# Modulation products on four column tiles of TensorE, six blocks summed in one PSUM bank, and the result turned by a product with a constant

## The reference

```python
for i in range(DEPTH):                      # second block, DEPTH = 2
    mod_l = (silu(c) @ w_mod[i] + b_mod[i]).reshape(b, 9, 1, 1024)
    mod_c = (silu(c_ctx) @ w_mod[i] + b_mod[i]).reshape(9, 1, 1024)
    x_lat = x_lat + 0.5 * mod_l[:, 2] * swiglu_2(modulate(x_lat, norm_gain[i, 0], mod_l[:, 0], mod_l[:, 1]), ...)
    h_l = modulate(x_lat, norm_gain[i, 1], mod_l[:, 3], mod_l[:, 4])
    ...                                     # even layer: attention and a long convolution; odd: retention
    x_lat = x_lat + mod_l[:, 5] * o_l
    x_lat = x_lat + 0.5 * mod_l[:, 8] * swiglu_2(modulate(x_lat, norm_gain[i, 2], mod_l[:, 6], mod_l[:, 7]), ...)
```

## Time and profile before

| | us |
|---|---|
| median of three runs | 3456.55 |
| lowest and highest of them | 3435.0 and 3467.14 |
| the profiled execution, its whole time | 3468.43 |
| its span from first to last instruction | 3466.6 |
| TensorE busy | 3324.8 |
| VectorE busy | 1682.6 |
| ScalarE busy | 1354.5 |
| modulation products (line 1065) | 293.0 |
| mean granted clock of TensorE | 0.974 |

### The profile page before, as it was taken

One profiled execution on the slowest core, in us unless ns is written; L12 is line 12 of the kernel. 1 busy time (PEld: TensorE's weight loads), 2 busy tenths in 40 slices (PEclk: granted clock), 3 DMA queues, 4 the chain that ended last, 5 costly groups with the idle time before them and its releaser, 6 DMA issues.

```text
span 3466.6 us, 45512 instructions
## 1 busy us (share of the span) xinstructions
PE 3324.8 (96%) x18258; PEld 2624.9 (76%) x18258; DVE 1682.6 (49%) x2742; ACT 1354.5 (39%) x2343; POOL 152.3 (4%) x177
## 2 busy tenths in 40 slices
PE   7999999999899999999999989999999999998899
PEld 6867959977595895888867436888868886885899
DVE  5655555566454655333374335433353345334565
ACT  3555454445544444222243523322242224233543
POOL 1110000002000000000010001000000000101000
PEclk8999999999999999999999899999999999999899
DMA  4444465553454655222342232322332324332454
GB/s 154 139 128 143 157 203 173 185 186 100 123 185 148 202 189 176 98 94 76 104 145 86 79 110 79 110 97 82 109 119 97 97 92 129 108 111 75 134 184 139
DMA packets 248950, 446.00 MB, mean 129 GB/s; under 512 B 16467, under 2 KB 56804, under 8 KB 247972
## 3 DMA queue, kind: packets, MB, share of 16 engines
q1 hardware_dynamic: 244656, 430.80, 38.7%
q10 hardware_dynamic: 4084, 12.29, 1.0%
HBM read 441.97 MB, written 1.05 MB: 128 GB/s over the span
## 4 chain that ended last, share of the span: by engine, by line
PE 86%; DVE 6%; ACT 3%; DMA 3%; issue 1%; POOL 0%; ACTq 0%; DVEq 0%; SPq 0%; POOLq 0%
PE bank L905 22%; PE bank L907 22%; PE bank L906 21%; PE bank L1065 5%; PE bank L1017 2%; PE bank L935 2%; PE bank L936 2%; PE bank L937 2%; PE bank L1032 2%; PE bank L864 1%; DMA mod<-w_mod 1%; DVE split L1531 1%; PE bank L1177 1%; ACT split L1252 1%; DVE A L1528 1%
## 5 line engine op out<-in xcount | busy, mean ns | idle before, releaser
L905 PE MATMUL bank<-AR,split 128*128 128x256 f32 (+1 forms) x4960 | 1624.0, 327 | 35.3 <-DVE A L1528 13.5
L907 PE MATMUL bank<-AR,split 128*128 128x256 f32 (+1 forms) x4960 | 1606.1, 324 | 0.0
L906 PE MATMUL bank<-AR,split 128*128 128x256 f32 (+1 forms) x4960 | 1601.6, 323 | 0.0
L1531 DVE TENSOR_TENSOR split<-raw,split 128x1024 fp32r<-128x1024 f32 (+2 forms) x712 | 806.5, 1175 | 912.8 <-ACT split L1252 911.4
L1252 ACT ACTIVATE split<-raw 128x1024 fp32r<-128x1024 f32 (+2 forms) x712 | 679.7, 1004 | 940.4 <-PE bank L907 833.2
L905 PEld LDWEIGHTS bank<-AR,split 128*128 128x128 f32 x4960 | 939.7, 189 | 140.7 <-DVE AR L1531 24.5
L906 PEld LDWEIGHTS bank<-AR,split 128*128 128x128 f32 x4960 | 940.4, 190 | 81.1 <-issue 1.7
L907 PEld LDWEIGHTS bank<-AR,split 128*128 128x128 f32 x4960 | 940.2, 190 | 78.0
L1065 PE MATMUL bank<-mod,lgs 128*2 128x512 f32 x576 | 293.0, 616 | 9.1 <-DMA mod<-w_mod 4.8
L1531 DVE TENSOR_TENSOR AR<-A,AR 128x256 fp32r<-128x256 f32 (+2 forms) x268 | 145.0, 543 | 52.9 <-ACT AR L1281 29.9
L1528 DVE SCALAR_TENSOR_TENSOR A<-A,bank 128x256 f32<-128x256 f32 (+1 forms) x196 | 97.0, 508 | 131.3 <-ACT A L1293 123.0
(11 more groups left out here) (214 smaller groups left out, 2158.5 us busy)
## 6 DMA issues: line engine op xcount, KB each, us to landing
mod<-w_mod SPq DMA_DIRECT2D x288, 256.0 KB, 2.8
raw<-w_in SPq DMA_DIRECT2D x120, 512.0 KB, 4.5
raw<-w_gu SPq DMA_DIRECT2D x80, 512.0 KB, 4.5
raw<-ffn_a_in SPq DMA_DIRECT2D x80, 512.0 KB, 4.4
raw<-ffn_b_in SPq DMA_DIRECT2D x80, 512.0 KB, 4.4
raw<-ret_in SPq DMA_DIRECT2D x48, 512.0 KB, 4.4
raw<-w_down SPq DMA_DIRECT2D x44, 512.0 KB, 4.8
raw<-ffn_a_out SPq DMA_DIRECT2D x44, 512.0 KB, 3.8
```

The source lines that it names most:

```text
L905: e.matmul(out, wh[:, c, m_], x.hi(k0 + c, a, b), start=first, stop=False)
L906: e.matmul(out, wh[:, c, m_], x.lo(k0 + c, a, b), start=False, stop=False)
L907: mm = e.matmul(out, wl[:, c, m_], x.hi(k0 + c, a, b), start=False, stop=last)
L1531: return self.e.tensor_tensor(out, v, hi.bitcast(F32), ALU.subtract)
```

## The change

A product of two columns uses 2 of the 128 columns of the array. The new code gives each of four chunks its own tile of 32 columns: chunk t of four writes partitions 32 t to 32 t + 31 of bank 7. Six blocks (a group, the six that one norm needs) are summed in the same bank. For this the stationary operand is a window of 32 columns out of a strip of zeros in which silu(c) of chunk k stands at columns 32 k + 10 and 32 k + 11; the window moves by two columns from block to block, so that block n fills rows 2 n and 2 n + 1 of each tile. When a group is complete, ScalarE copies all 128 partitions, and TensorE multiplies them by a constant 128 x 12 matrix with four stacked unit matrices, which at once sums the four tiles and turns the result. VectorE adds the bias for 24 columns at a time.

Steps still come one by one, but only each fourth has work: four products, and on SyncE the four loads of the next batch after a wait for the whole batch. `settle` is gone, since bank 7 belongs to the modulation; other users share banks 0 to 6.

```diff
-PROJ, ROT, STAT, MODP = (0, 1, 2, 3), (4, 5), 5, (6, 7)
-BESIDE, APART = ((3, 4, 5), (6,), (7,)), ((4, 1, 2), (3,), (0,))
+PROJ, ROT, STAT, MODB = (0, 1, 2, 3), (4, 5), 5, 7
+BESIDE, APART = ((3, 4), (5,), (6,)), ((4, 1, 2), (3,), (0,))
-ALL = tuple(range(8))
+ALL = tuple(range(7))
...
-    def settle(self):
-        while self.mod_step % 8 and self.mod_step < 288:
-            next(self.filler)
-
-    def mods_done(self):
-        return 36 if self.mod_step > 288 else max(0, (self.mod_step - 4) // 8)
+    def groups_done(self):
+        return 6 if self.mod_step > 288 else max(0, (self.mod_step - 4) // 48)
 
     def modulations(self):
-        for i in range(2):
-            for nb in range(18):
+
+        for g in range(6):
+            for n in range(6):
                 for c in range(8):
                     self.mod_step += 1
-                    self.mod_tile(i, nb, c)
-                    if c == 3 and self.mod_step > 8:
-                        self.mod_finish(*divmod(i * 18 + nb - 1, 18))
+                    if g == n == c == 0:
+                        self.mod_start()
+                    if c % 4 == 3:
+                        self.mod_four(g, n, c - 3)
+                    if g and n == 0 and c == 3:
+                        self.mod_finish(g - 1)
                     yield
         self.mod_step += 1
-        self.mod_finish(1, 17)
+        self.mod_finish(5)
         yield
...
-    def mod_tile(self, i, nb, c):
-        e, f, q = self.e, ("mod", i, nb), (i * 18 + nb) * 8 + c
-        if q == 0:
-            e.wait_ge(*self.after("c"))
-        if c == 0:
-            self.fresh(f, (MODP[nb % 2],))
-        e.wait_ge(*self.after(("mod load", q)))
-        s3 = self.mem["lgs"][:, 64:80].rearrange("p (c s) -> p c s", s=2)
-        mm = e.matmul(self.bank(f)[0:2, :], s3[:, c, :], self.mem["mod"][q % MODS][:, :], start=c == 0, stop=c == 7)
-        mm.then_inc(*self.mark(("mod used", q), *([("full", f)] if c == 7 else [])))
-
-    def mod_finish(self, i, nb):
-        f = ("mod turn", i, nb)
+    def mod_four(self, g, n, c):
+        e, f = self.e, ("mod", g)
+        if n == c == 0:
+            self.fresh(f, (MODB,))
+        for t in range(4):
+            k = (g * 6 + n) * 8 + c + t
+            e.wait_ge(*self.after(("mod load", k)))
+            at = (c + t) * 32 + 10 - 2 * n
+            mm = e.matmul(self.bank(f)[32 * t:32 * t + 32, :], self.mem["strip"][:, at:at + 32], self.mem["mod"][t][:, :], start=n == c == 0, stop=n == 5 and c == 4)
+        mm.then_inc(*self.mark(("mod used", g, n, c), *([("full", f)] if n == 5 and c == 4 else [])))
+
+    def mod_start(self):
+        self.e.wait_ge(*self.after("c"))
+
+    def mod_finish(self, g):
+        f = ("mod turn", g)
         out = self.fresh(f, (STAT,))
-        self.e.wait_ge(*self.after(("mod row", i, nb)))
+        self.e.wait_ge(*self.after(("mod row", g)))
         for m in range(4):
-            mm = self.turn(out[:, 2 * m:2 * m + 2], self.mem["mrow"][0:2, m * P:(m + 1) * P])
+            mm = self.e.matmul(out[:, 12 * m:12 * m + 12], self.mem["mrow"][:, m * P:(m + 1) * P], self.base[:, 512:524], start=True, stop=True)
         mm.then_inc(*self.mark(("full", f)))
...
-    def mod_tile(self, i, nb, c):
-        q = (i * 18 + nb) * 8 + c
-        for k in range(0 if q == 0 else q + MODS - 1, min(288, q + MODS)):
-            if k >= MODS:
-                self.e.wait_ge(*self.after(("mod used", k - MODS)))
-            self.e.dma_start(self.mem["mod"][k % MODS][:, :], self.io["w_mod_2"][k // 144][k % 8 * P:(k % 8 + 1) * P, k // 8 % 18 * 512:(k // 8 % 18 + 1) * 512]).then_inc(
-                *self.mark(("mod load", k), on=f"m{k % MODS}", by=16))
+    def mod_start(self):
+        self.load_four(0)
+
+    def mod_four(self, g, n, c):
+        q = ((g * 6 + n) * 8 + c) // 4 + 1
+        if q < 72:
+            self.load_four(q)
+
+    def load_four(self, q):
+        e = self.e
+        if q:
+            e.wait_ge(*self.after(("mod used", (q - 1) // 12, (q - 1) // 2 % 6, (q - 1) % 2 * 4)))
+        for t in range(4):
+            k = 4 * q + t
+            e.dma_start(self.mem["mod"][t][:, :], self.io["w_mod_2"][k // 144][k % 8 * P:(k % 8 + 1) * P, k // 8 % 18 * 512:(k // 8 % 18 + 1) * 512]).then_inc(
+                *self.mark(("mod load", k), on=f"m{t}", by=16))
```

More of the change, by code:

```diff
@@ L57, in constants @@
     heads[64:, 64:] = 1.0 / 64
-    out["base"] = np.concatenate([eye, rot32, rot64, heads], axis=1)
+    pick = np.zeros((128, 12), f32)
+    for j in range(4):
+        pick[32 * j:32 * j + 12] = np.eye(12, dtype=f32)
+    out["base"] = np.concatenate([eye, rot32, rot64, heads, pick], axis=1)
     pos = np.arange(NT, dtype=f32)
@@ L156, in stat @@
             k = self.sets.get("at", 0)
-            k = 0 if k + n > 512 else k
+            k = 0 if k + n > 256 else k
             self.small[key] = k
@@ L647, in even @@
         self.load_hyena()
-        self.settle()
         self.turn_z()
@@ L719, in modulation @@
     def modulation(self, i, j):
-        while self.mods_done() < 18 * i + 6 * (j + 1):
+        while self.groups_done() < 3 * i + j + 1:
             next(self.filler)
@@ L841 @@
     load_lambda = load_context = load_window = load_hyena = load_axial = load_decay = await_context = nothing
-    mod_tile = mod_finish = gains = normed = conv = q_gain = hyena_z = turn_z = filter_layer = filter_end = nothing
+    mod_start = mod_four = mod_finish = gains = normed = conv = q_gain = hyena_z = turn_z = filter_layer = filter_end = nothing
     filter_spectra = convolution = axial = silu_out = log_gamma = decay = nothing
@@ L1181, in ret_gate @@
         f = ("rt", hd, qt)
-        out = self.fresh(f, (6, 7))
+        out = self.fresh(f, (6,))
         self.e.wait_ge(*self.after(("ret y", hd, qt)))
@@ L1739, in subln, with mod_start, mod_finish @@
             self.low(self.AR[:, pair.l + a:pair.l + b], v, self.AR[:, pair.h + a:pair.h + b]).then_inc(*self.mark((pair.name, 2 * half), (pair.name, 2 * half + 1)))
-    def mod_tile(self, i, nb, c):
+    def mod_start(self):
         e, g = self.e, self.mem["lgs"]
-        if i == nb == c == 0:
-            e.wait_ge(*self.after("c tanh"))
-            self.stt(g[:, 80:96], g[:, 80:96], 1.0, self.cl("c", 0, 16), ALU.add, ALU.mult).then_inc(*self.mark("c twice"))
-            e.wait_ge(*self.own())
-            e.tensor_scalar(g[:, 64:80], g[:, 80:96], 0.5, None, ALU.mult).then_inc(*self.mark("c"))
-    def mod_finish(self, i, nb):
-        f = ("mod turn", i, nb)
+        e.wait_ge(*self.after("c tanh"))
+        self.stt(g[:, 80:96], g[:, 80:96], 1.0, self.cl("c", 0, 16), ALU.add, ALU.mult).then_inc(*self.mark("c twice"))
+        e.wait_ge(*self.own())
+        e.wait_ge(*self.after("strip"))
+        e.tensor_scalar(self.mem["strip"][:, 10:266].rearrange("p (c n) -> p c n", c=8)[:, :, 0:2], g[:, 80:96].rearrange("p (c s) -> p c s", c=8), 0.5, None, ALU.mult).then_inc(*self.mark("c"))
+    def mod_finish(self, g):
+        f, i, a = ("mod turn", g), g // 3, g % 3 * 24
         self.e.wait_ge(*self.after(("full", f)))
+        b = self.bank(f)[:, 0:48].rearrange("p (m n s) -> p n m s", m=4, n=6)
+        out = self.modt[i][:, a:a + 24, :].rearrange("p (n m) s -> p n m s", n=6)
+        bias = self.cl("b_mod", i * 72 + a, 24).rearrange("p (n m) -> p n m", n=6)
         for s in range(2):
-            self.e.tensor_tensor(self.modt[i][:, nb * 4:nb * 4 + 4, s], self.bank(f)[:, 0:8].rearrange("p (m s) -> p m s", s=2)[:, :, s],
-                                 self.cl("b_mod", i * 72 + nb * 4, 4), ALU.add).then_inc(*self.mark(*([("free", f)] if s else [])))
+            self.e.tensor_tensor(out[:, :, :, s], b[:, :, :, s], bias, ALU.add).then_inc(*self.mark(*([("free", f)] if s else [])))
     def gains(self, i, j):
@@ L1976, in start @@
         e.memset(self.epsc[:, :], EPS).then_inc(*self.mark("eps"))
+        e.memset(self.mem["strip"][:, :], 0.0).then_inc(*self.mark("strip"))
     def await_tables(self):
@@ L2125, in build @@
         mem["split"] = [sb(f"split{i}", 2 * 4 * 512, dt=F32R) for i in range(SPLIT)]
-        for name, n in (("base", 512), ("ones", 128), ("cols", NCOLS), ("small", 512), ("epsc", 1), ("mods", 288), ("gsc", 48), ("lgs", 96), ("mrow", 512)):
+        for name, n in (("base", 524), ("strip", STRIP), ("ones", 128), ("cols", NCOLS), ("small", 256), ("epsc", 1), ("mods", 288), ("gsc", 48), ("lgs", 96), ("mrow", 512)):
             mem[name] = sb(name, n)
```

19 lines of the change are left out of this document (7 added, 12 removed).

## The result

The changed kernel takes **3522.62 us**, the median of four runs (3515.2 to 3527.83). The kernel before, run beside it, takes 3454.52 us (3435.0 to 3467.14). The ratio is 1.0201, with a 95% interval of 1.0149 to 1.0253, so the change makes the kernel slower by 1.5% to 2.5%. The prediction said 3453 us and a range from 3405 to 3505; the measured time lies above it. The medians are 68.1 us apart. The profiled executions' spans are 3526.0 us against 3466.6 before, 59.4 us apart: the profiled execution of the kernel before (3468.43) was 13.9 us slower than its median, that of the changed kernel (3527.83) 5.2 us. What follows accounts for the 59.4.

A forecast was written before the change was run, and what follows sets the result against it. TensorE was taken as the bound in attention, with products on its path, and loads in norm stops. Terms -45 - 3 + 10 + 19.5 + 5 + 10 = -3.5 us moved the median 3456.55 to 3453 us; range 3405 to 3505.

The forecast's parts named there:

- settling: Ahead of pipelines near 760 and 2016 us: products drained to close a group of eight are gone, -3 us.
- SyncE's queue: Ahead of the cross attention: w_o_x's request waits behind the batch's loads, 2.5 us later, twice, +5 us.
- Attention: Five attention stretches: shorter products and fewer turns save 49.5 us, 4 given back for blocking TensorE, net -45 us.
- Clock: Norm stops: idle TensorE lowers the clock, half of ten stops lose about 2 us, +10 us, bounds 0 and 35.
- the turn-round of 5.5 us: Norm stops and last stop: 1.05 us to a batch's signal plus 4.45 us until its fourth load lands.
- Norm stops: Ten stops around norms: four requests wait for the whole batch, together 206.4 us against 196.2, +10 us.
- The last stop: Stop at 3263.86 us: four leftover batches stand ahead of its ones sums, 18.7 us, with copy and turns +19.5 us.
- What bounds the kernel: TensorE, busy 96% of the span; products lie on its path in attention, while loads decide in norm stops.
- A batch of four, 2.24 us: Four products side by side: eight MATMULs take five slots, since only neighbouring products' second and first overlap; chance 0.50.
- Rival 1: Every batch: all four products run at once, 0.95 to 1.2 us a batch, total 3410 us; chance 0.18.
- rival 3: Stops: turn-round decides; 6.85 us each gives +36 and 3489 us, loads of 4.3 give 3421; chance 0.10.
- Everything else: Row copies, bias additions and the strip's memset: nothing of this is on a path, 0 us.

The follow-up runs named there:

- own_step: The changed kernel with one product a step, each in its own column tile, each buffer refilled when its own product is over: 3493.89 us, ratio 1.0107.
- pairs: The changed kernel with batches of two products, each second step, in two column tiles, the next pair already loaded: 3462.34 us, ratio 1.0033.
- shift32: The kernel before with 32 unused columns ahead of the arena A, which puts A at the changed kernel's address: 3455.65 us, ratio 1.0002.
- shift: The kernel before with 22 unused columns ahead of the arena A, nothing else changed: 3480.21 us, ratio 1.0083.

## Why the prediction was wrong, step by step

Of the 62.9 us between the predicted -3.5 and the measured +59.4, attention with settling and SyncE's queue has 31.0 (-43 predicted, -12.0 measured), the ten stops with the clock term 16.6 (+20, +36.6), the last stop 6.8 (+19.5, +26.3) and the projections 8.5 (0, +8.5). So the terms that failed are *Attention*, together with *Clock*, which let the low clock into the stops only, and the turn-round of 5.5 us in *Norm stops* and *The last stop*.

1. *What bounds the kernel* was right: products on the path in attention, loads in the stops.
2. *A batch of four, 2.24 us*: wrong, it is 0.99. The failed step is "The second must follow the first, so only the second of one product and the first of the next overlap". In the trace's records four MATMULs of a batch, one of each product (each stands beside a weight load that waits for another buffer), start some 7 ns apart (1989.93 to 1989.95), and the other four 0.45 us later. So a product's second MATMUL does not hold up the next tile's first; whether the engine lets them pass or they reach it in this order, the trace doesn't show. Rival 1's short batch held, and its 3410 us didn't: with the right batch the rest of the working would have missed by more, so the long batch hid a part of the other errors. The Trainium skill, "TensorE: Matmul & The Clock Gate", section "Part 3: Packing small matmuls — row/col tiling", gives 2.38 times for three column tiles; the runs show 3.6 times for four (3.56 over 0.99).
3. *Attention, -45*: wrong in the rest of the chain. TensorE's work fell by more than I assumed, yet the stretches give -12.0. I let the clock into the stops only, and named as a sign of being wrong "if the clock stayed low through attention": that is what happened in the first block. There, 72 products of 0.95 became 18 batches of 0.99, 50.6 us less work. Half-clock time grew by 104 us, of which 9 fell into idle time; the other 95 cost 44 at the 0.46 above. The later w_o_x adds 7. And TensorE's other waits, mostly for VectorE, grew from 0.8 to 14.9 us, where the prediction had given back 4 for all of attention. By these estimates that makes +14.5; measured are +12.2. In the second block's stretch, where half-clock time hardly changes (44.4 to 51.2, worth 3 us), some 40 us of work are gone and TensorE's idle time grows by 14 (20.3 to 34.1, most of it in the convolution): 27.1 us are given back, part of them by chance, as said above.
4. *Settling, -3*: right for the two products near 760 us. From the projection MATMUL ahead of them to the one behind them it was 3.3 us before and is 1.5 in the changed kernel. The one near 2016 wasn't measured apart.
5. *Ten norm stops, +10*: the mechanism was right, the size wrong. The failed term is the turn-round of 5.5 us: I had measured 5.8 us to the fourth landing at 240 us, and took off 1.3 for a 512 KB load ahead of it. The time is 5.6 without that load, so the subtraction was wrong, and rival 3's 1.05 + 5.8 was the nearer value. It had put 36 us more on the eleven stops than the prediction did; measured are 33.4 more (26.6 and 6.8). With 6.7 to 7.6 us a batch the ten stops cost +36.6; own_step and pairs, with 201.5 and 199.4, show that it is the requests in a block of four that wait for one event.
6. *The last stop, +19.5*: right in kind and place, measured +26.3. From the first batch's start to the last one's end it is 23.1 us (3303.16 to 3326.24) in place of 18.7, again the turn-round (6.8 and 6.7 us in place of 5.5), and 22 us of the stop are at 1.2 GHz.
7. *SyncE's queue, +5*: right. The wait ahead of the cross attention grew from 2.46 and 2.43 to 6.03 and 5.87 us, +7.0, and falls back with own_step.
8. *Clock, +10*: far too small, with the wrong bounds (0 to 35) and the wrong place. Half-clock time rose from 180 to 390 us over the span. What it costs in the stops, where TensorE is idle for 103 of 268 us, no run shows apart; in the first block's attention it costs about 44 us, by the estimate of step 3.
9. *Everything else, 0*: one thing was missing, the address of A. It moved the 512-wide projections by +7 us three times and gave as much back elsewhere (shift32, 1.0002). So the projections' +8.5 us aren't shown to be its work: shift32, with the same address, has 17.8 us less than the changed kernel, and 11 of them lie in the start, ahead of the first attention (245.4 us against 234.2, half-clock time 27.3 against 17.1). In the kernel before the start took 242.1, so one execution's start scatters by about that much.

Put together: a product more than three times cheaper was bought with 37 us of turn-round, 26 us of leftovers and 7 us of a late load, and of what attention should have given, the low clock kept about half (by the estimates of step 3, 47 us of 91) and TensorE's longer waits a further part. What stays open is why batches of two leave the clock at 2.4 GHz in the first block's first and third stretch and batches of four don't; the runs show that they do (three traces of each, with one exception among the pairs), not what in the spacing of the work decides it.

## What to carry to other kernels

Before filler work is made cheaper, ask what it keeps alive: where the engine was busy without a break at 2.4 GHz only because of it, price the stretch at 1.2 GHz too. A row of the profile before can have the price: here the two cross attentions, 28.7 us at 1.00 and 36.5 at 0.77. And when several buffers are freed by one event in place of several, count the turn-round of the whole block of loads, not of one, and look for the place where the rest of the steps ends up. Packing pairs kept the rolling loads and most of the packing's gain.

## What the runs showed of the hardware that I had not expected

- Eight fp32 MATMULs of 512 columns on four column tiles take as long as two on one, 0.99 us against 0.95; in one tile they take 3.56.
- Four 256 KB loads requested together from one queue land in 5.6 us (median of 72), with a gap of 1.6 us between the second and the third in the case shown; single ones land in 2.5 to 2.7.
- The address of the arena that MATMULs read sets the steady spacing of the 512-wide ones: 228.9, 234.3, 233.3 and 226.7 ns at 120512, 120608, 120640 and 120704 B, the same in every kernel with that address. Unused columns alone cost 0.8% (shift) or nothing (shift32).
- The time that a stretch full of TensorE's work loses at 1.2 GHz is 0.46 us for each us there, in two pairs of stretches with the same work.
